# Packing the modulation rows of two to four chunks into one PSUM bank, with changed orders at block 1's passes and spare transposes ahead of block 2

## The chip, the core and the metric

The kernel runs on one core of one Trainium2 chip. The metric is the device time of one launch in microseconds (us). Three runs of the kernel before took 1881.89, 1884.19 and 1881.85 us, so the median is 1881.89 us.

## What is computed

Two blocks follow each other on 256 tokens of width 1024, everything in float32. Block 1 has two layers with a side input `ctx`, of 256 tokens too. Each layer first makes the modulation from the conditioning vectors (one for `x`, one for `ctx`), then a wide projection whose columns feed a retention branch, a differential attention branch and a gated MLP branch:

```python
for l in range(DEPTH):
    shift, scale, gate = split((silu_c @ w_mod[l] + b_mod[l]), 3)        # for x
    shift_c, scale_c, gate_c = split(silu_cc @ w_mod[l] + b_mod[l], 3)   # for ctx
    h  = rms_norm(x, g_pre[l]) * (1 + scale) + shift
    hc = rms_norm(ctx, g_pre[l]) * (1 + scale_c) + shift_c
    # ctx: projections hc @ w_in[l] (all columns in layer 0, four groups in layer 1),
    #      final retention states s_f, s_b = sum_j gamma^(..) k_j v_j^T per head
    # x:   projections h @ w_in[l], rotation of q and k, retention from s_f, s_b,
    #      differential attention over ctx keys and own keys, chunk MLP
    x = x + gate * rms_norm(merge(o_ret, o_mlp, o_diff) @ w_out[l], g_post[l])
```

Block 2 has two layers of three attention branches and a squared-ReLU MLP. The change touches of it only the transposes of `x` with which its first layer begins.

## The kernel before

**Products.** A float32 product is made of three products of parts (lines 1620, 1621 and 1622: high by high, high by low, low by high). Weights come in slabs of 256 rows by 512 columns through four slots. SyncE loads a slab into `raw`, ScalarE (ACT) rounds it to the high part `whi` (line 523), GpSimd (POOL) subtracts to get the low part `wlo` (line 498), and TensorE (PE) uses both. Four slabs make a chunk of 512 output columns for 256 tokens in two banks. Each engine has its own program, written out by hand, and waits on counting semaphores; the order of the instructions in each program is the order of the work.

**Passes.** Block 1 runs four passes: 0 is `ctx` of layer 0, 1 is `x` of layer 0, 2 is `ctx` of layer 1 (four column groups only), 3 is `x` of layer 1. Banks are named `A[0..3]` and `G[0..3]`. The slabs accumulate in `G`; `A` holds transposes, states and scores.

**Modulation.** `mod_slab` (PE, line 1739) multiplies one slab of `w_mod` with the silu of the conditioning vectors, stored two columns wide in blocks of 32 columns of zeros (`cond`). It gives two useful rows in each of four groups of 32 partitions of a bank. A chunk of `w_mod` takes four such slabs; there are 12 chunks. ScalarE copies the bank out (`mod_copy`, line 684), and `mod_turn` (line 1748) sums the row groups and turns them into columns: four products of two columns for each chunk. Chunks 0 to 3 run at the start, each in a bank of its own (`A[0], A[1], G[0], G[1]`) with its copy and its turn behind it; chunks 4 and 5 run beside pass 0's first two chunks of `w_in`, chunks 6 to 9 beside its next four, chunks 10 and 11 beside pass 1's third and fourth. The rows of chunks 6 to 11 wait in six buffers, and 24 products turn them at one place in pass 1.

**States.** In passes 0 and 2 VectorE (DVE) scales the values of four heads (`state_values`, line 1303), PE sums them per head (`sum_states`, line 1859) into four banks, and ScalarE copies each bank (line 784). In pass 0 the scaled values have room for two heads, so the third head waits for the first sum. PE waits for all four copies before the retention scores (line 1945).

**Decay matrices.** `decays` takes for each head two exponentials on ScalarE (lines 714 and 715) and three operations of 128x512 on VectorE (1282 to 1284). For layer 1, heads 0 and 1 are built at the end of pass 1, heads 2 and 3 at the end of pass 2 (ScalarE) and the start of pass 3 (VectorE).

**Edges between passes.** The normed tokens are transposed by `turn_tokens` (line 1686) in four quarters through `A[2]` and `A[3]`; ScalarE makes the high part (line 586) and VectorE the low part (1102 and 1105). Slab q of the next pass needs quarter q. Before pass 3, PE turns quarters 0 and 1 after the second and third slab of pass 2's last chunk, and 2 and 3 once both are split.

**Differential attention.** Around each of eight steps run three slabs of later columns (`late_slab`). When the fourth slab of a chunk is done, ScalarE copies two banks (line 559) before PE may start the next chunk there. ScalarE's exponentials (line 851) stand ahead of these.

**Start of block 2.** `turn_by_token` (line 1696) transposes each token tile of `x` as soon as `last_residual` has closed it (line 1147).

Of the kernel before, what the change touches and what calls it, by code (L numbers as in the profile page):

```python
# [27 lines left out]
P = 128  # L28
# [9 lines left out]
W = 512  # L38
# [47 lines left out]
def constants():  # L86
# [17 lines left out]
    pick = np.zeros((2, 2, 32, 2, 2), np.float32)  # L104
    for h in range(2):
        for a in range(2):
            pick[h, :, a, h, a] = 1
# [35 lines left out]
def build(nc, g, out):  # L143
# [14 lines left out]
    with ExitStack() as ctx:  # L158
# [73 lines left out]
        modkeep = sb_at("modkeep", [P, 4, MODN], F32, place["gate2_5"])  # L232
        modlast = sb("modlast", [P, 2, MODN])
        modkept = [modkeep[:, m] for m in range(4)] + [modlast[:, m] for m in range(2)]
# [10 lines left out]
        pick = cst["pick"].rearrange("p (h a) -> p h a", h=2)  # L245

        modw = sb("modw", [P, MODW, SLAB_K, CH])
        modrow = sb_at("modrow", [P, 4, MODN], F32, eb)
        moddrop = sb_at("moddrop", [P, 2, MODN], F32, place["aT"])
        cT = sb("cT", [P, KT, 2])  # L250
        cond = sb("cond", [P, KT, 32])
# [52 lines left out]
        OUT = [A[2], A[3]]  # L304
        UP = [[G[0], G[1]], [A[0], A[1]]]
# [207 lines left out]
        def _(act):  # L513
# [157 lines left out]
            act.activation(cond[:, :, 0:2], cT[:], ACT.Silu).then_inc(silu_c, 1)  # L671
# [9 lines left out]
            def mod_copy(bank, dst):  # L681

                act.wait_ge(mod_used, w(mod_used, SLOTS))
                act.activation(dst, bank[:, 0:MODN], ACT.Copy).then_inc(mod_copied, 1)
# [6 lines left out]
            for n, (is_x, l, full) in enumerate(PASSES):  # L691
                if n == 0:
                    act.wait_ge(ctx_in, w(ctx_in, 16))
                    norm(cx)
                    for c in range(4):
                        mod_copy((A[0], A[1], G[0], G[1])[c], modrow[:, c])
# [3 lines left out]
                stream_high(n, range(4) if n == 0 else (2, 3))  # L700
# [17 lines left out]
                if is_x:  # L718
                    pass_by(0)
                else:  # L720
                    evacuate(0, columns(z, RK), ACT.Copy)
                if n == 0:
                    mod_copy(A[2], moddrop[:, 0])
                    setup_rest()
# [25 lines left out]
                def beside_ctx_dv(s):  # L750
# [3 lines left out]
                    elif s < SLOTS - 1:  # L754
# [3 lines left out]
                        stream_high(3, (s - 1,))  # L758
# [12 lines left out]
                if n == 0:  # L771
                    mod_copy(A[3], moddrop[:, 1])
# [18 lines left out]
                if n == 0:  # L791
                    mod_copy(A[2], modkept[0])
# [6 lines left out]
                if n == 1:  # L799
                    mod_copy(A[0], modkept[4])  # L800
                if n == 2:
# [3 lines left out]
                    decays((2, 3), l)  # L805
# [4 lines left out]
                if n == 0:  # L810
                    mod_copy(A[3], modkept[1])
# [1452 lines left out]
```

## Time and profile before

| what | value |
|---|---|
| the profiled execution, its own time | 1882.96 us |
| its span | 1881.0 us |
| PE / weight loads | 98% / 81% of the span |
| POOL, ACT, DVE | 72%, 56%, 36% |
| share of the last chain that is PE's | 92% |
| DMA over the whole span | 174 GB/s; 354 and 307 GB/s in the first two of 40 slices |

The span is the stretch between the first and the last instruction of the profile; the execution's own time is some 2 us longer. Busy PE is not PE at its peak: the end of a matmul is modelled, and the rate is read from the distance of the starts. A product in float32 without parts (lines 1739, 1748, 1859, 1945) shows two records for each call, a transpose (1686, 1696, 1867) one.

### The profile page before, as it was taken

What the parts mean: (1) busy time and instruction counts of PE and PEld (TensorE: products, weight loads), DVE (VectorE), ACT (ScalarE), POOL (GpSimd) and SP (SyncE); (2) the same over time, 40 slices, a digit from 0 to 9 for tenths busy, and PEclk for the clock granted to TensorE, in tenths of its full rate; (3) what the DMA queues carried; (4) which work ended last, traced back from release to release, by engine and by line L of the source; (5) the groups of instructions that cost most, each with busy time, mean ns of one, the idle gap of its engine ahead of it and who ended that gap; (6) DMA issues with size and microseconds to landing.
All of it is one profiled execution on the core that took longest, in us unless ns stands there. A gap on an engine that the chain in (4) does not pass through costs nothing.

```text
span 1881.0 us, 26575 instructions
## 1 busy us (share of the span) xinstructions
PE 1841.7 (98%) x9988; PEld 1525.6 (81%) x9988; DVE 682.1 (36%) x1149; ACT 1045.0 (56%) x1551; POOL 1360.2 (72%) x573
## 2 busy tenths in 40 slices
PE   6999999999999999999999999999999999999998
PEld 3668888778788787878878887889998887789997
DVE  3432444512335755132434382321111745231112
ACT  3554675534667663455755666654445576645444
POOL 3567778856668778666877765778887965678886
PEclk8999999999999999999999999999999999999999
DMA  9875555754446556545555543456555654356553
GB/s 354 307 240 145 159 167 179 239 156 143 145 141 202 168 158 189 146 144 147 173 158 174 168 143 116 156 170 189 189 189 157 206 149 124 123 168 202 190 186 128
DMA packets 171416, 328.52 MB, mean 175 GB/s; under 512 B 10416, under 2 KB 15792, under 8 KB 171184
## 3 DMA queue, kind: packets, MB, share of 16 engines
q1 hardware_dynamic: 168272, 320.49, 54.8%
q10 hardware_dynamic: 3040, 6.58, 1.0%
q8 instruction: 74, 1.21, 0.3%
q14 instruction: 30, 0.25, 0.0%
HBM read 325.98 MB, written 1.05 MB: 174 GB/s over the span
## 4 chain that ended last, share of the span: by engine, by line
PE 92%; DVE 4%; ACT 2%; issue 1%; DMA 1%; SPq 0%; DVEq 0%; ACTq 0%
PE G L1620 22%; PE G L1622 21%; PE G L1621 21%; PE G L2200 2%; PE A L2202 2%; PE G L2202 2%; PE A L2201 2%; PE G L2201 2%; PE A L2200 2%; PE A L1620 2%; PE A L1621 2%; PE A L1622 2%; PE A L1981 1%; PE A L1739 1%; PE G L2004 1%
## 5 line engine op out<-in xcount | busy, mean ns | idle before, releaser
L498 POOL TENSOR_TENSOR wlo<-raw,whi 128x1024 fp32r<-128x1024 f32 (+1 forms) x568 | 1356.5, 2398 | 506.9 <-ACT whi L523 505.5
L523 ACT ACTIVATE whi<-raw 128x1024 fp32r<-128x1024 f32 (+1 forms) x568 | 594.1, 1048 | 623.7 <-PE G L1622 492.3
L1620 PE MATMUL G<-whi,hhi 128*128 128x512 f32 (+1 forms) x1488 | 597.0, 401 | 13.8 <-DVE hlo L1105 7.6
L1622 PE MATMUL G<-whi,hlo 128*128 128x512 f32 (+1 forms) x1488 | 577.6, 388 | 0.0
L1621 PE MATMUL G<-wlo,hhi 128*128 128x512 f32 (+1 forms) x1488 | 577.3, 388 | 0.0
L1620 PEld LDWEIGHTS G<-whi,hhi 128*128 128x128 f32 x1488 | 281.2, 189 | 86.0 <-issue 27.2
L1622 PEld LDWEIGHTS G<-whi,hlo 128*128 128x128 f32 x1488 | 281.1, 189 | 59.2
L1621 PEld LDWEIGHTS G<-wlo,hhi 128*128 128x128 f32 x1488 | 281.8, 189 | 50.8
L1620 PE MATMUL G<-whi,osplit 128*128 128x512 f32 x240 | 94.2, 393 | 0.0
L1621 PE MATMUL G<-wlo,osplit 128*128 128x512 f32 x240 | 93.5, 389 | 0.0
L1622 PE MATMUL G<-whi,osplit 128*128 128x512 f32 x240 | 93.4, 389 | 0.0
L1406 DVE TENSOR_REDUCE nmx<-A 128x1 f32<-128x512 f32 (+1 forms) x48 | 26.7, 597 | 135.6 <-PE A L1981 135.6
L2200 PE MATMUL G<-hhi,whi 128*128 128x256 f32 x256 | 72.5, 283 | 2.6 <-DVE hlo L1108 2.6
L2202 PE MATMUL A<-hhi,wlo 128*128 128x256 f32 x256 | 72.4, 283 | 0.0
L2201 PE MATMUL A<-hlo,whi 128*128 128x256 f32 x256 | 72.4, 283 | 0.0
L2202 PE MATMUL G<-hhi,wlo 128*128 128x256 f32 x256 | 72.4, 283 | 0.0
L2201 PE MATMUL G<-hlo,whi 128*128 128x256 f32 x256 | 72.4, 283 | 0.0
L2200 PE MATMUL A<-hhi,whi 128*128 128x256 f32 x256 | 72.4, 283 | 0.0
L559 ACT ACTIVATE z<-G 128x512 f32<-128x512 f32 x66 | 38.8, 598 | 27.1 <-PE G L1622 27.1
L1620 PEld LDWEIGHTS G<-whi,osplit 128*128 128x128 f32 x240 | 45.1, 188 | 9.5 <-issue 0.3
L1622 PEld LDWEIGHTS G<-whi,osplit 128*128 128x128 f32 x240 | 45.1, 188 | 9.5
L1621 PEld LDWEIGHTS G<-wlo,osplit 128*128 128x128 f32 x240 | 45.1, 188 | 9.0
(400 smaller groups left out, 2547.4 us busy)
## 6 DMA issues: line engine op xcount, KB each, us to landing
raw<-in_w_in SPq DMA_DIRECT2D x324, 512.0 KB, 3.7
raw<-in_w_up SPq DMA_DIRECT2D x64, 512.0 KB, 3.7
raw<-in_w_down SPq DMA_DIRECT2D x64, 512.0 KB, 3.6
raw<-in_w_out SPq DMA_DIRECT2D x40, 512.0 KB, 3.6
raw<-in_w_branch_out SPq DMA_DIRECT2D x36, 512.0 KB, 3.9
modw<-in_w_mod SPq DMA_DIRECT2D x32, 512.0 KB, 5.1
raw<-in_w_branch SPq DMA_DIRECT2D x24, 512.0 KB, 3.5
modz<-in_w_mod SPq DMA_DIRECT2D x16, 512.0 KB, 9.7
```

The source lines that it names most:

```text
L498: pool.tensor_tensor(wlo[:, s, :, 0:n], raw[:, s, :, 0:n], whi[:, s, :, 0:n].bitcast(F32), ALU.subtract)\
L523: act.activation(whi[:, slot, :, 0:n], raw[:, slot, :, 0:n], ACT.Copy).then_inc(hi_ready, 1)
L559: act.activation(dst[c][t], banks[t][:], func, scale=1.0 if scale is None else scale[t])\
L1406: ins = dve.reduce_max(nmx[:, i % 2, b:b + 1], A[2 * (i % 2) + b][:, 0:nk], AX.X, negate=True)
L1620: pe.matmul(bank, hi, whi[:, slot, kk, 0:n], start=first, stop=False)
L1621: pe.matmul(bank, hi, wlo[:, slot, kk, 0:n], start=False, stop=False)
L1622: return pe.matmul(bank, lo, whi[:, slot, kk, 0:n], start=False, stop=last)
L1739: ins = pe.matmul(bank[at:at + 32, 0:MODN], cond[:, q * SLAB_K + kk], ring[:, i % size, kk, h * MODN:(h + 1) * MODN], start=q == 0, stop=q ...
L1981: ins = pe.matmul(bank[:, c * S:(c + 1) * S], dqT[half_p, h, t * P:(t + 1) * P], kT[half_p, h], start=True, stop=True)
L2200: pe.matmul(part, high, hhi[:, k], start=k == 0 and f % 2 == 0, stop=False, skip_group_check=True)
L2201: pe.matmul(part, high, hlo[:, k], start=False, stop=False, skip_group_check=True)
L2202: ins = pe.matmul(part, low, hhi[:, k], start=False, stop=last, skip_group_check=True)
```

## The change

Chunks of `w_mod` that are copied together accumulate in one bank: chunks 0 to 3 in `G[0]`, 4 and 5 in `A[2]`, 6 and 7 in `A[3]`, 8 and 9 in `A[2]`, 10 and 11 in `A[0]`. The c-th chunk of a group reads `cond` two columns further left for each c, so its two rows land at rows 2c and 2c+1 of each group of 32, and adds to the bank. One copy and two products serve a group, each of 16 columns for four chunks and 8 for two. That makes 10 products instead of 48, and 5 copies instead of 12.

The orders that change: states go two heads to a bank, with two copies of 128x512 for four of 128x256, and the scaled values have room for four heads; PE waits for these copies one step later in pass 0. Heads 0 and 1 of layer 1's decay are finished by VectorE in pass 2 and at the start of pass 3, heads 2 and 3 after the first and third rotation of pass 3; ScalarE makes the exponentials of 2 and 3 after pass 3's first chunk. The transposes before pass 3 come one slab earlier and three quarters of them lie inside pass 2. ScalarE closes a chunk ahead of its exponentials where the chunk's last slab comes first in a step. And the first layer of block 2 gets 20 and 10 spare transposes, whose output nothing reads.

```diff
-            pick[h, :, a, h, a] = 1
+            for c in range(4):
+                pick[h, :, 2 * c + a, c, h, a] = 1
...
-                    for c in range(4):
-                        mod_copy((A[0], A[1], G[0], G[1])[c], modrow[:, c])
+                    mod_copy(G[0], modrow, 4)
...
-                stream_high(n, range(4) if n == 0 else (2, 3))
+                stream_high(n, (range(4), (2, 3), (2, 3), (3,))[n])
...
                 if is_x:
                     pass_by(0)
+                    if n == 3:
+                        decays((2, 3), l)
...
-                        stream_high(3, (s - 1,))
+                    stream_high(3, (s,)) if s < SLOTS - 1 else None
...
-                    for h in range(H1):
+                    for b, bank in enumerate(STATE_BANKS[n]):
                         act.wait_ge(state_sum, w(state_sum))
-                        act.activation(state[:, h].rearrange("p d n -> p (d n)"), A[h % 4][:, 0:2 * DK1], ACT.Copy,
+                        act.activation(state[:, 2 * b:2 * b + 2].rearrange("p h d n -> p (h d n)"), bank[:], ACT.Copy,
...
                 if n == 2:
                     act.wait_ge(x_updated, w(x_updated))
                     norm(x)
                     copy_states()
-                    decays((2, 3), l)
...
+                    closes = i < m and late % SLOTS == SLOTS - 1
+                    if closes:
+                        late_slab(late, late_dst, G[2:4])
+                        late += 1
                     if i < m:
                         act.wait_ge(diff_max, w(diff_max))
...
-                        for _ in range(2):
+                        for _ in range(1 if closes else 2):
...
-                stream_low(n, range(4) if n == 0 else (2, 3))
+                stream_low(n, (range(4), (2, 3), (2, 3), (3,))[n])
...
                 if n == 3:
-                    decays((2, 3), l)
+                    decays((1,), l)
...
-                        if h >= 2 and full:
-                            dve.wait_ge(state_sum, w(state_sum))
...
                 if n == 2:
                     residual(x)
+                    decays((0,), l)
                     dve.wait_ge(evacuated, w(evacuated, 4 * TT))
                     state_values()
                     norm(x)
-                    stream_low(3, (0, 1))
+                    dve.wait_ge(state_sum, w(state_sum, 2))
+                    stream_low(3, (0, 1, 2))
...
+                        if n == 3 and c in (0, 2):
+                            decays((2 + c // 2,), l)
...
                 if n == 1:
                     dve.wait_ge(tables_in, w(tables_in, 16 * N_TABLE[1]))
-                    decays((0, 1), 1)
...
-            def turn_by_token(src, banks):
+            def turn_by_token(src, banks, spare=(0, 0)):
...
+                    for n in range(spare[t]):
+                        k = n % KT
+                        pe.transpose(G[2 * t][:, n % 4 * P:(n % 4 + 1) * P], src[:, 0, k * P:(k + 1) * P], ident)
...
-                        ins = pe.matmul(bank[at:at + 32, 0:MODN], cond[:, q * SLAB_K + kk],
-                                        ring[:, i % size, kk, h * MODN:(h + 1) * MODN], start=q == 0,
-                                        stop=q == SLOTS - 1, skip_group_check=True)
+                        ins = pe.matmul(bank[at:at + 32, 0:MODN], cond[:, 8 + 32 * (q * SLAB_K + kk) - 2 * c:][:, 0:32],
+                                        ring[:, i % size, kk, h * MODN:(h + 1) * MODN], start=q == 0 and c == 0,
+                                        stop=q == SLOTS - 1 and c == last, skip_group_check=True)
...
-                for b in range(CH // P):
-                    h, j = divmod(b, 2)
-                    ins = pe.matmul(bank[:, at + 2 * b:at + 2 * b + 2], src[:, j * P:(j + 1) * P], pick[:, h],
-                                    start=True, stop=True)
+                turned_rows = bank[:, at:at + 8 * chunks].rearrange("p (c j a) -> p j c a", j=2, a=2)
+                for j in range(2):
+                    ins = pe.matmul(turned_rows[:, j], src[:, j * P:(j + 1) * P], pick[:, 0:2 * chunks], start=True, stop=True)
...
+                else:
+                    pe.wait_ge(h_split, w(h_split))
+                    turn_tokens(normed, HB_EDGE, (3,))
...
                         if s == 0:
-                            pe.wait_ge(state_copied, w(state_copied, H1))
                             turn_ws()
+                            pe.wait_ge(norm_ready, w(norm_ready, TT))
+                            pe.wait_ge(state_copied, w(state_copied))
...
-                            turn_tokens(normed, HB_EDGE, (s - 1,))
+                            if s == 2:
+                                pe.wait_ge(h_split, w(h_split))
+                        if s < SLOTS - 1:
+                            turn_tokens(normed, HB_EDGE, (s,))
...
-                                for b in range(6):
-                                    mod_turn(A[2], 8 * b, modkept[b], b == 5)
+                                for b in range(3):
+                                    mod_turn(A[2], 16 * b, modkept[b], last=b == 2)
...
                 if n == 0:
                     sum_states()
-                    pe.wait_ge(state_copied, w(state_copied, H1))
 
                 for i in range(H1 + 1):
+                    if n == 0 and i == 1:
+                        pe.wait_ge(state_copied, w(state_copied, 2))
+                        pe.wait_ge(mod_copied, w(mod_copied))
...
-                turn_by_token(x, HB_DOWN if l else HB_OUT)
+                if l == 0:
+                    turn_by_token(x, HB_OUT, (20, 10))
+                else:
+                    turn_by_token(x, HB_DOWN)
```

## Rows read from the trace of the kernel before

**Rows 1.** The page, its part 1: busy time, share of the span, instructions.

```profile
PE 1841.7 (98%) x9988; PEld 1525.6 (81%) x9988; DVE 682.1 (36%) x1149; ACT 1045.0 (56%) x1551; POOL 1360.2 (72%) x573
```

**Rows 2.** The waits of PE, whole span: total us, times, longest us.

```profile
PE G L1620 <- DVE hlo L1105: 7.6, 3, 5.6
...
PE G L1620 <- ACT z L559: 2.0, 4, 0.5
PE A L1686 <- DVE hlo L1105: 1.7, 1, 1.7
PE G L1620 <- DVE z L1340: 1.4, 1, 1.4
```

**Rows 3.** Windows: length, busy by engine, granted PE clock, DMA share, GB/s.

```profile
396.00:408.00 12.00, 12.00 (x69) 10.73 (x68) 0.62 (x4) 1.95 (x3) 2.81 (x2) 0.72 0.31 90
...
980.00:995.00 15.00, 11.25 (x46) 8.92 (x45) 7.61 (x16) 10.95 (x24) 9.36 (x4) 0.78 0.31 81
```

**Rows 4.** Timeline, pass 1's turns: start, us, engine, line, operation.

```profile
396.38 3.63 PE L1748 MATMUL A<-const,modkeep 128*128 128x2 f32 x32
...
402.09 0.77 PE L1620 MATMUL G<-whi,hhi 128*128 128x512 f32 x1
...
408.04 0.49 PE L1620 MATMUL G<-whi,hhi 128*128 128x512 f32 x1
...
411.26 0.48 PE L1620 MATMUL G<-whi,hhi 128*128 128x512 f32 x1
```

**Rows 5.** Timeline, pass 0's turns of chunks 4 and 5.

```profile
68.38 1.97 PE L1748 MATMUL A<-const,moddrop 128*128 128x2 f32 x16
...
68.87 0.38 ACT L684 ACTIVATE moddrop<-A 128x256 f32<-128x256 f32 x1
...
70.21 0.49 PE L1620 MATMUL G<-whi,hhi 128*128 128x512 f32 x1
```

**Rows 6.** Timelines of DVE and PE, pass 0's states and first scores.

```profile
113.91 3.80 DVE L1303 TENSOR_SCALAR e<-z,reachv 128x128 f32<-128x128 f32 x8 [9.88 <-ACT z L538]
...
129.06 0.64 PE L1739 MATMUL A<-modw,cond 128*32 128x256 f32 x8
...
131.03 1.99 PE L1859 MATMUL A<-e,z 128*128 128x256 f32 x8 [1.34 <-ACT modkeep L684]
...
136.32 1.13 PE L1945 MATMUL A<-tT 128*128 128x256 f32 x4 [0.47 <-ACT state L784]
...
137.10 0.58 PE L1620 MATMUL G<-whi,hhi 128*128 128x512 f32 x1
```

**Rows 7.** Timelines of DVE, PE and ACT around pass 2.

```profile
637.62 2.89 DVE L1283 TENSOR_TENSOR e<-e,dist 128x512 f32<-128x512 f32 x1
...
681.68 1.42 DVE L1086 TENSOR_SCALAR normed<-x,rstd 128x1024 f32<-128x1024 f32 x2
...
683.28 0.60 PE L1844 MATMUL A<-const,wsin 128*128 128x128 f32 x4
...
682.50 1.28 ACT L714 ACT_TABLE_LOAD   x1
...
686.26 1.04 ACT L523 ACTIVATE whi<-raw 128x1024 fp32r<-128x1024 f32 x1
```

**Rows 8.** Timeline of PE at the start of block 2.

```profile
983.36 1.04 PE L1696 MATMUL A<-const,x 128*128 128x128 f32 x8
...
986.75 1.09 PE L1696 MATMUL A<-const,x 128*128 128x128 f32 x8 [2.35 <-DVE x L1147]
...
989.25 0.77 PE L1620 MATMUL G<-whi,hhi 128*128 128x512 f32 x1 [1.41 <-DVE hlo L1108]
...
994.93 0.48 PE L1621 MATMUL G<-wlo,hhi 128*128 128x512 f32 x1
```

**Rows 9.** Timeline of PE at the start: two runs of eight transposes.

```profile
24.52 1.66 PE L1686 MATMUL A<-const,normed 128*128 128x128 f32 x8
...
26.02 1.04 PE L1686 MATMUL G<-const,normed 128*128 128x128 f32 x8
```

More of the change, by code:

```diff
@@ L231, in build @@
         gate2_5 = sb("gate2_5", [P, TT, CH])
-        modkeep = sb_at("modkeep", [P, 4, MODN], F32, place["gate2_5"])
-        modlast = sb("modlast", [P, 2, MODN])
-        modkept = [modkeep[:, m] for m in range(4)] + [modlast[:, m] for m in range(2)]
+        modkept = [sb_at(f"modkept{m}", [P, MODN], F32, place["gate2_5"] + m * MODN * 4) for m in range(3)]
         modT = sb("modT", [P, 2, KT, 2])
@@ L304, in build @@
         OUT = [A[2], A[3]]
+        STATE_BANKS = {0: [A[3], A[1]], 2: [A[2], A[3]]}
         UP = [[G[0], G[1]], [A[0], A[1]]]
@@ L679, in tables, with mod_copy @@
                 act.dma_start(wsins[l][:], g["mlp_w_s"][l].rearrange("a i j -> i a j")).then_inc(tables_in, 16)
-            def mod_copy(bank, dst):
-                act.wait_ge(mod_used, w(mod_used, SLOTS))
-                act.activation(dst, bank[:, 0:MODN], ACT.Copy).then_inc(mod_copied, 1)
+            def mod_copy(bank, dst, chunks=2):
+                act.wait_ge(mod_used, w(mod_used, chunks * SLOTS))
+                act.activation(dst[:], bank[:, 0:MODN], ACT.Copy).then_inc(mod_copied, 1)
             def setup_rest():
@@ L1306, in state_values @@
                         ins.then_inc(state_v, 1)
-                    dve.wait_ge(state_sum, w(state_sum, 2 if full else H1))
                 if n == 2:
                     residual(x)
+                    decays((0,), l)
                     dve.wait_ge(evacuated, w(evacuated, 4 * TT))
@@ L1732, in mod_slab @@
                 mods["n"] += 1
+                c = i // SLOTS
+                c, last = (c, 3) if c < 4 else (c % 2, 1)
                 ring, full, size = (modz, modz_full, MODZ) if i < 4 * SLOTS else (modw, modw_full, MODW)
@@ L1848, in _ @@
                     turn_ws()
-                    for c in range(2):
-                        pe.wait_ge(mod_copied, w(mod_copied))
-                        mod_turn(A[1], 8 * c, moddrop[:, c], c == 1)
+                    pe.wait_ge(mod_copied, w(mod_copied))
+                    mod_turn(A[1], 0, moddrop)
                 def sum_states():
@@ L1856, in sum_states @@
                         for t in range(TT):
-                            values = e[:, h % 2, t, 0:2 * DK1] if full else z[:, h // 2, (RQ, DQ)[h % 2]:(RQ, DQ)[h % 2] + W].rearrange(
+                            values = e[:, h % 2, t, h // 2 * 2 * DK1:(h // 2 + 1) * 2 * DK1] if full else z[:, h // 2, (RQ, DQ)[h % 2]:(RQ, DQ)[h % 2] + W].rearrange(
                                 "p (t n) -> p t n", t=TT)[:, t]
-                            ins = pe.matmul(A[h][:, 0:2 * DK1], z[:, t, RK + h * DK1:RK + (h + 1) * DK1],
-                                            values, start=t == 0, stop=t == TT - 1)
-                        ins.then_inc(state_sum, 1)
+                            ins = pe.matmul(STATE_BANKS[n][h // 2][:, h % 2 * 2 * DK1:(h % 2 + 1) * 2 * DK1],
+                                            z[:, t, RK + h * DK1:RK + (h + 1) * DK1], values, start=t == 0, stop=t == TT - 1)
+                        if h % 2 == 1:
+                            ins.then_inc(state_sum, 1)
                 def turn_group(bank, blocks):
```

58 lines of the change are left out of this document (24 added, 34 removed).

## The prediction, made before the changed kernel was run

> **What bounds the kernel now.** I read the page's busy times first [rows 1]. PE is busy 98% of the span, POOL 72%, ACT 56%. So each microsecond of PE work that goes, and each wait of PE that goes, comes off the end, as long as its suppliers keep pace; work moved on the other engines is free while PE does not wait for it. The waits of PE come second [rows 2]. After the start, where 5.6 of the 7.6 us on the low part `hlo` (line 1105) lie, the largest are few and all near the change: 2.0 us for `hlo` at the start of pass 2, 1.7 at the start of pass 3, 1.4 for the first rotation of pass 3, 2.0 for four bank copies in the attention. Third come the windows with their granted clock [rows 3]. It is 0.72 over 396 to 408 us and 0.78 over 980 to 995, so in both PE ran for a part at 1.2 GHz and for the rest at 2.4. Last I read the timelines of these places for what PE did just before [rows 4 to 9].
>
> **Part 1, pass 1's turns.** 24 products, 48 records, run from 396.38 to 402.09: 5.71 us, 0.119 each [rows 4]. Of these 12 records stay. A record of 8 moving columns instead of 2 is not in the trace. Its price lies between 0.119 us and the 0.2 us of a state product with 256 columns (eight records in 1.99 us, of which about 0.4 is the end of the last) [rows 6]; so 1.4 to 2.4 us. I take 1.4, since 8 is nearest to 2. Gain 4.3 us. Behind the turns the clock has fallen: the slab and four transposes from 402.09 to 408.04 take 5.95 us, the next slab with its transposes 3.22 (408.04 to 411.26) [rows 4]. That is 2.7 us more. Does it go? In pass 0, 16 such records took 1.97 us and the slab behind them starts with a record of 0.49 us, the length of the one at 408.04 at full clock [rows 4, 5]. So 1.97 us of narrow products did not lower the clock there, and 1.4 should not. Gain 7.0 us together.
>
> **Part 2, pass 0's turns.** Here 16 records become 4, but PE cannot take all of it. The single copy now waits for the second chunk, and that copy ran from 68.87 to 69.25 [rows 5]. With 4 records at 0.12 behind it the next slab starts at 69.8 instead of 70.21 [rows 5]. Gain 0.4 us.
>
> **Part 3, the start.** Three of the four turns there lie between slabs of `w_mod`, which arrive by DMA, and the last turn goes from 8 records to 4 (0.5 us by the price above). But `hhi` on ACT and `hlo` on DVE stand behind it together with the first weight slabs, whose transfers have not changed. I set 0, with bounds of 1.0 us worse (the first slab later because fewer products leave PE at the low clock longer) and 1.5 better (the last turn's 0.5 us and its successors in step).
>
> **Part 4, pass 0's states and scores.** Now the last modulation slab starts at 129.06, the copy holds PE 1.34 us, states of two heads run, a wait for the third head's values, two more heads, 0.47 us for the state copy, scores at 136.32 and the slab at 137.10 [rows 6]. After: nothing of this is waited for. The values of all heads are early: eight scalings took 3.80 us from 113.91 [rows 6], so sixteen end near 122, and nothing before 129 wants them. The copies are asked for one step later, behind two slabs. So PE goes from 129.7 (129.06 + 0.64) through 16 state records at 0.2 (3.2 us) and the scores (137.10 - 136.32 = 0.8) to the slab at 133.7. Gain 3.4 us.
>
> **Part 5, edges of passes 2 and 3.** The decay work of heads 0 and 1 stood on DVE ahead of pass 2's low parts. One of its six operations took 2.89 us at 637.62, while POOL ran [rows 7]; without them the 2.0 us wait [rows 2] has no cause. Head 0's three operations now come after `residual`; at 2.89 each they take up to 8.7 us, and the values they delay are needed only when the second chunk is done. Before pass 3 the quarters are turned one slab earlier, and the 1.7 us wait [rows 2] goes, since its quarter has then a whole slab of time. DVE's two decays before the first rotation become one, 8.7 us less at that price, so the 1.4 us wait [rows 2] goes. Gain 2.0 + 1.7 + 1.4 = 5.1 us. What is added: PE waits in pass 2 for the normed tokens after the first slab and the turn of `w_s`. Those are ready at 683.10 (681.68 + 1.42), and PE is there at about 683.6, after the turn that starts at 683.28 [rows 7]. It costs nothing with 0.5 us of margin; queued behind it are all later slabs. ACT gets a table load and four exponentials in pass 3, in front of its next slab: they took 3.8 us in pass 2 (682.50 to 686.26), and PE did not wait then [rows 2, 7]. Those of head 3 wait until DVE has built head 1, 8.7 us at worst. No SyncE instruction moves; POOL's order is the same, it follows ACT.
>
> **Part 6, attention.** In passes 1 and 3 a chunk's last slab comes first in two of the eight steps: four places, the four waits of 2.0 us in all [rows 2]. ACT's copies now precede its exponentials. The exponentials come later by a slab at most, and their sum is used one step (three slabs) later. Gain 2.0 us.
>
> **Part 7, spare transposes.** The eight transposes at 983.36 are followed by 2.35 us of waiting, those at 986.75 by 1.41, and then the clock is low: from 989.25 to 994.93 run 13 records in 5.68 us [rows 8]. At full clock one is 0.228 us (3.22 less 0.48 for four transposes, over 12) [rows 4], so 13 cost 2.97; the low clock costs 2.7 us. Eight transposes take 1.04 us with the end of the last in it [rows 8], some 0.11 each. Twenty take 2.2 us and fill the first gap, ten take 1.1 and lie in the second, where their successors already have their signal. If the gaps were shorter than I read, each spare transpose would cost its 0.11 us: 0.3 us in all if the first gap is overrun. Do they hold the clock? At the start PE's clock was low at 24.52 (eight transposes in 1.66 us) and full for the eight at 26.02 (1.04 us) [rows 9]; so a run of transposes, behind narrow products, did raise it. I take the 2.7 us as gained.
>
> The Trainium skill speaks against this part: "TensorE: Matmul & The Clock Gate", Part 4 (PE-mode transpose), says that full clock does not engage for transposes, which do not count as PE activity in the same way. By that rule the sum would lose this term. The two runs at 24.52 and 26.02 speak against the rule, though slabs stood just before them.
>
> **The sum.** 7.0 + 0.4 + 0 + 3.4 + 5.1 + 2.0 + 2.7 = 20.6 us. The profiled execution took 1882.96 us for a span of 1881.0, so it would be near 1862.4. It was 1.07 us above the median of 1881.89, and the median after should be 1861.3 us, 1.1% less.
>
> **The rivals.** *The spare transposes do not hold the clock.* For it: they are half as dense in columns as a slab, and eight plus eight of them did not hold it [rows 8]. Against it: the gaps were open then, and rows 9. Everything else holds: 1861.3 + 2.7 + up to 0.3, or 1864.2.
>
> *New waits take the place of the old ones in block 1's last passes.* The 0.5 us margin on the normed tokens is thin, and ACT's moved exponentials stand before slabs while DVE's operations run at 2.89 instead of 0.7 us when POOL is busy [rows 7]. The 5.1 us of part 5 come back, and 1 us of part 4: 1867.4.
>
> *The start turns well or the clock falls at other places.* The three runs before lie 2.3 us apart, which is about one such stretch of low clock. At best 1857 with 1.5 us at the start and one low stretch less.
>
> *The change does not do what it says:* the waits are put down to the wrong releaser, and behind each stands another (a slab's low part from POOL). Then only the products' own 4.7 us of parts 1 and 2 go, less new waits of 2: about 1879.
>
> *Slower.* ACT's program stops in pass 3 ahead of its slab until DVE has built head 1, and all four heads' decays come onto the path that way or behind the rotations: 12 operations at 2.89, 35 us, less some 3 us of slab in store (the 3.8 us that did no harm in pass 2). 1861.3 + 32 = 1893. It decides only where these waits exceed 20.6 us; up to the slack nothing is seen. Against it: DVE idles between the rotations, since each waits for a chunk of four slabs.
>
> **How the numbers follow.** Forecast with all parts 0.52; spare transposes without effect 0.24; new waits 0.13; a better start 0.05; not what it says 0.04; slower 0.02. Only the last lies above 1881.89, and 0.2% of it, 3.8 us, is about what a measurement of this kernel can tell from no change; 1879 lies within. So faster 0.94, same 0.04, slower 0.02. The forecast's own range is 1858.5 to 1863.5 (bounds of part 3, 1.0 us for wider products, one clock stretch). With the second and third case the range is 1857 to 1868.
>
> **What would show it.** Line 1748 has 20 records instead of 96, and in pass 1 the next slab starts with a record near 0.49 us, not 0.77. Pass 0's first late slab starts 4 us after its last modulation slab, not 8. PE waits on lines 1686, 1620 (`hlo` near 650, `z` of line 1340) and 1859 are gone, and none over 0.5 us comes at the move of `norm_ready`. After the spare transposes the first slab of block 2 starts with a record near 0.5 us, not 0.77. The prediction is wrong if POOL or a transfer stands behind PE at one of these places, if the clock falls elsewhere, or if the start grows longer.

## The result and the profile after

The changed kernel takes 1865.82 us (median of four runs, 1864.62 to 1865.95), the kernel before on the same chip 1881.87 us. The ratio is 0.991, with a 95% interval of 0.990 to 0.992: 16.05 us less. The forecast was 1861.3, so 4.5 us of the expected gain are missing. The profiled execution took 1864.62 us for a span of 1862.7, against 1882.96 and 1881.0. The measured time lies above the range of 1858.5 to 1863.5 that the forecast gave for itself, and within the range of 1857 to 1868 that takes in two of its rivals. By the spans the gain is 18.3 us; the profiled execution before lay 1.1 us above its median, that after 1.2 us below. The accounts below are made in the spans. The lines have moved: the slab products are now lines 1619 to 1621, `mod_slab` 1743, `mod_turn` 1752, `sum_states` 1860, `turn_tokens` 1685, `turn_by_token` 1695 and its spare transposes 1700, `hlo` 1103 and 1106, `state_values` 1299.

The waits of PE over the whole span (total us, times, longest us), to be read beside [rows 2]:

```profile
PE G L1619 <- DVE hlo L1103: 6.1, 1, 6.1
PE A L1860 <- DVE z L1299: 3.9, 1, 3.9
...
PE G L1619 <- DVE hlo L1106: 1.7, 2, 1.3
```

The four waits for bank copies, the quarter's wait before pass 3, the rotation's wait and the 2.0 us for `hlo` at the start of pass 2 are gone. One wait of 3.9 us is new: the state sums of pass 2 wait for the scaled values. Here are the places of the change in the timeline of PE (start, us, engine, line, operation, what it waited for), to be read beside [rows 4, 5, 6, 8]:

```profile
68.48 0.61 PE L1752 MATMUL A<-const,moddrop 128*128 128x8 f32 x4 [0.75 <-ACT moddrop L684]
68.95 0.49 PE L1619 MATMUL G<-whi,hhi 128*128 128x512 f32 x1
...
127.80 0.64 PE L1743 MATMUL A<-modw,cond 128*32 128x256 f32 x8
128.37 3.72 PE L1860 MATMUL A<-e,z 128*128 128x256 f32 x16
131.93 1.03 PE L1951 MATMUL A<-tT 128*128 128x256 f32 x4
132.60 0.58 PE L1619 MATMUL G<-whi,hhi 128*128 128x512 f32 x1
...
391.91 1.40 PE L1752 MATMUL A<-const,modkept 128*128 128x8 f32 x12
393.17 0.48 PE L1619 MATMUL G<-whi,hhi 128*128 128x512 f32 x1
...
396.36 0.48 PE L1619 MATMUL G<-whi,hhi 128*128 128x512 f32 x1
...
661.23 1.02 PE L1860 MATMUL A<-z 128*128 128x256 f32 x4
666.18 4.26 PE L1860 MATMUL A<-z 128*128 128x256 f32 x12 [3.93 <-DVE z L1299]
670.10 0.58 PE L1619 MATMUL G<-whi,hctx 128*128 128x512 f32 x1
...
684.25 0.48 PE L1619 MATMUL G<-whi,hhi 128*128 128x512 f32 x1
...
968.73 2.35 PE L1700 MATMUL G<-const,x 128*128 128x128 f32 x20
...
972.17 1.25 PE L1700 MATMUL G<-const,x 128*128 128x128 f32 x10
973.74 0.47 PE L1619 MATMUL G<-whi,hhi 128*128 128x512 f32 x1 [0.32 <-DVE hlo L1106]
```

Where the time went is read by the start of the same PE instruction in both traces, and the lead grown between two of them:

| from one place to the next | before | after | lead grows by | forecast |
|---|---|---|---|---|
| first slab of pass 0 | 37.16 | 37.16 | 0 | 0 |
| its last modulation slab beside `w_in` chunk 1 | 67.32 | 66.51 | 0.81 | 0 |
| slab behind pass 0's turns | 70.21 | 68.95 | 0.45 | 0.4 |
| first late slab of pass 0, behind the states | 137.10 | 132.60 | 3.24 | 3.4 |
| slab behind pass 1's turns | 402.09 | 393.17 | 4.42 | 4.3 |
| next slab (the low clock) | 408.04 | 396.36 | 2.76 | 2.7 |
| states of pass 2 (attention copies, `hlo`) | 677.09 | 661.23 | 4.18 | 1.0 + 2.0 |
| slab behind these states | 680.36 | 670.10 | **-5.60** | 0 |
| second slab of pass 3 (the quarter) | 696.45 | 684.25 | 1.94 | 1.7 |
| slab behind the first rotation | 744.92 | 730.98 | 1.74 | 1.4 |
| first slab of block 2 (attention copies) | 989.25 | 973.74 | 1.57 | 1.0 |
| to the end (the low clock) | 1881.0 | 1862.7 | 2.8 | 2.7 |

Eleven rows lie at the forecast, within 0.2 us below it, or above it, and one gives 5.6 us back, at a place where the sum had put nothing. Its window (length, busy us of PE, PEld, DVE, ACT and POOL with their counts, granted clock, DMA share, GB/s) shows that PE was at the low clock for part of it:

```profile
661.23:670.10 8.87, 4.94 (x18) 3.79 (x16) 7.96 (x15) 4.62 (x8) 4.62 (x2) 0.81 0.69 207
```

### The profile page after: what moved, and what is told of

It is laid out like the page before. It is cut to its first block, busy times and chain, and to the rows that moved or that the text cites. A ratio compares the mean times of both kernels' runs of the same rounds, so it can differ in the third digit from the quotient of the medians.

```text
span 1862.7 us, 26472 instructions
## 1 busy us (share of the span) xinstructions
PE 1829.0 (98%) x9942; PEld 1515.8 (81%) x9942; DVE 692.3 (37%) x1149; ACT 1042.5 (56%) x1540; POOL 1360.2 (73%) x573
## 3 DMA queue, kind: packets, MB, share of 16 engines
HBM read 325.98 MB, written 1.05 MB: 176 GB/s over the span
## 4 chain that ended last, share of the span: by engine, by line
PE 94%; DVE 2%; DMA 1%; ACT 1%; issue 1%; SPq 0%; DVEq 0%; ACTq 0%
PE G L1619 23%; PE G L1621 22%; PE G L1620 22%; PE G L2209 2%; PE A L2211 2%; PE A L2210 2%; PE G L2211 2%; PE G L2210 2%; PE A L2209 2%; PE A L1619 2%; PE A L1620 2%; PE A L1621 2%; PE A L1987 1%; PE G L2010 1%; PE A L1743 1%; PE A L1673 1%
```

## The experiments

Each kernel is the changed one with one edit, if nothing else is said. The kernel before was timed on the same chip beside each group: 1882.18 us beside e1 to e4, 1881.96 beside e5 to e8 and 1882.08 beside e9 to e11.

### Why pass 2 gave 5.6 us back

DVE's timeline in pass 2, changed kernel. The three operations of head 0's decay stand at 639.66 to 647; then come the scalings:

```profile
644.31 2.77 DVE L1282 TENSOR_TENSOR decay<-e 128x512 f32<-128x512 f32 x1
651.18 16.52 DVE L1299 TENSOR_SCALAR z<-z,reachv 128x128 f32<-128x128 f32 x16 [4.10 <-ACT z L538]
```

And POOL's, which runs without a gap from 636.13 to 665.85:

```profile
636.13 29.72 POOL L498 TENSOR_TENSOR wlo<-raw,whi 128x1024 fp32r<-128x1024 f32 x12 [4.20 <-ACT whi L523]
```

In the kernel before, the same sixteen scalings started at 667.04 and took 11.93 us. How many of them are done in a stretch is read from the windows of that line alone (length, DVE busy and count, clock, DMA share, GB/s). A window counts every operation that touches it, so one that crosses an edge is counted on both sides:

```profile
651.18:653.50 2.32, 2.32 (x2) 1.00 0.78 224
653.50:656.00 2.50, 2.50 (x2) 1.00 0.73 224
...
663.20:665.85 2.65, 2.65 (x2) 0.96 0.84 242
665.85:667.70 1.85, 1.84 (x10) 0.50 0.73 214
```

The seven windows from 651.18 to 667.70 (the three not shown count two each) count 22 operations, and each of their six inner edges is crossed by one. So seven of the sixteen scalings start while POOL runs, one for each of its operations, and the other nine follow in 1.85 us once POOL has stopped. The timeline from 651.75 shows two of the slow ones:

```profile
651.70 4.81 DVE L1299 TENSOR_SCALAR z<-z,reachv 128x128 f32<-128x128 f32 x2
```

The kernel before had a gap of POOL from 667.23 to 668.03. Five scalings start in the 1.03 us up to its end. In the 7.35 us of three POOL operations behind it four start, three of which take 2.4 to 2.5 us each; the fifth that this window counts crosses its edge:

```profile
667.00:668.03 1.03, 0.99 (x5) 1.00 0.70 265
668.03:675.38 7.35, 7.35 (x5) 1.00 0.63 177
```

*Theory:* beside POOL each of DVE's short operations lasts as long as the POOL operation next to it, and POOL ran dry less, because PE no longer stood still for 2.0 us at the pass's start. *Rival:* head 0's decay, moved ahead of the scalings, simply delays them.

**Head 0's decay behind the norm** (e3_decay0_later).

```diff
                     residual(x)
-                    decays((0,), l)
                     dve.wait_ge(evacuated, w(evacuated, 4 * TT))
                     state_values()
                     norm(x)
+                    decays((0,), l)
```

> Head 0's three decay operations on VectorE move from ahead of pass 2's 16 value scalings to behind the norm of x. Two causes are told apart for the new wait of 3.9 us of the state products for the scalings (16.5 us where they took 11.9 before). Theory A (POOL runs without a gap because PE's wait at the start of pass 2 is gone, and each pair of scalings waits for a 2.4 us subtraction): the wait stays at 3 to 4 us, span 1862 to 1863. Theory B (the decay operations ahead slow POOL and push its work into the scalings): scalings near 12 us, the wait gone, span near 1857.5.

Measured: 1863.08 us (1862.85 to 1864.17), 2.7 less than the changed kernel. The scalings still took 15.63 us from 652.09, beside eleven POOL operations in a row (26.14 us from 637.03), one gap of POOL of 0.79 us (663.17 to 663.95), in which four scalings start, and one more operation. PE's waits were 2.7 us in two:

```profile
663.40 1.96 PE L1860 MATMUL A<-z 128*128 128x256 f32 x8 [1.10 <-DVE z L1299]
666.99 1.99 PE L1860 MATMUL A<-z 128*128 128x256 f32 x8 [1.62 <-DVE z L1299]
```

So the moved decay explains a part of the loss, the smaller one of the waits (3.9 to 2.7). The rest stays with the decay out of the way. That the clock no longer fell beside the shorter waits (16 records in 3.95 us of work, against 4.26 us for the last 12) makes up the other part of the gain.

**Four scalings in place of sixteen** (e4_four_scalings). The same values, in four operations of 128x512 with a broadcast factor:

```diff
+                    if not full:
+                        dst4 = z[:, :, RQ:RQ + 4 * W].rearrange("p a (b c n) -> p a b c n", b=2, n=DK1)
+                        for t in range(TT):
+                            for d in range(2):
+                                ins = dve.tensor_tensor(dst4[:, :, :, 2 * t + d], ..., ALU.mult)
+                        ins.then_inc(state_v, H1)
+                        return
```

> Pass 2's 16 scalings of 128x128 become four tensor_tensor operations of 128x512 with a broadcast factor. Theory A (what costs is that every second operation waits for a subtraction of POOL): four operations take at most 4 x 2.9 = 11.6 us, more likely 6 to 9, ready before PE asks 10 us after the copy; the 3.9 us wait and the slow state products behind it go, 5.6 us in all, span near 1857.1. Rival (something else stands ahead of the state products, x_updated or the transfers): the wait stays, span near 1862.7.

Measured: 1860.86 us (1860.21 to 1861.27), 5.0 less than the changed kernel. DVE and PE:

```profile
651.87 9.47 DVE L1298 TENSOR_TENSOR z<-z,reachv 128x512 f32<-128x512 f32 x4 [4.11 <-ACT z L538]
```

```profile
661.92 3.61 PE L1871 MATMUL A<-z 128*128 128x256 f32 x16
665.18 0.58 PE L1630 MATMUL G<-whi,hctx 128*128 128x512 f32 x1
...
669.51 0.66 PE L1696 MATMUL A<-const,normed 128*128 128x128 f32 x4 [0.81 <-DVE normed L1084]
```

The first took 1.05 us and the other three 2.9 each, one to a POOL operation, with the decay still ahead of them. A short scaling beside POOL had taken 2.4. So it is the number of operations that cost, much more than their columns. The wait is gone, and what was next late is the thing the prediction had given 0.5 us of margin: the normed tokens, by 0.8 us. The span of 1858.8 us is 1.7 above the 1857.1 expected: 1.0 at the normed tokens, and 0.7 at the start, where the clock rose later than in the changed kernel's profile.

**The decays back at the end of pass 1** (e5_decays_back). This puts the 2.0 us wait back:

```diff
-                if n == 3:
-                    decays((1,), l)
...
                     residual(x)
-                    decays((0,), l)
...
                     dve.wait_ge(tables_in, w(tables_in, 16 * N_TABLE[1]))
+                    decays((0, 1), 1)
```

> VectorE builds the decays of heads 0 and 1 at the end of pass 1 again, as in the kernel before; nothing of them is left in pass 2 or at the start of pass 3. All else is the changed kernel's. Theory A (GpSimd without gaps): the wait of 2.0 us for hlo at the start of pass 2 comes back and lets GpSimd run dry once per slab, so its subtractions there stand in groups with gaps between; the 16 scalings take some 12 us instead of 16.5, TensorE doesn't wait 3.9 us for them, and the state records don't run at the low clock. That is 5.6 us gained for 2.0 lost: about 1862.3, although a wait was put back. Theory B (only the three decay operations ahead of the scalings matter): without them 2.7 us are gained, as when they stood behind the scalings (1863.1), and the returned wait costs 2.0: about 1865, with scalings still near 15.6 us and a wait for them of 1 to 2.7 us. If the scalings' length has nothing to do with either, the time is 1867.8.

Measured: 1861.98 us (1861.39 to 1862.54), 3.8 *less* than the changed kernel, with a wait more in it; theory A had 1862.3. PE, then POOL, then DVE:

```profile
636.06 0.47 PE L1617 MATMUL G<-whi,hhi 128*128 128x512 f32 x1 [1.77 <-DVE hlo L1103]
...
663.92 3.61 PE L1858 MATMUL A<-z 128*128 128x256 f32 x16
```

```profile
643.98 7.35 POOL L498 TENSOR_TENSOR wlo<-raw,whi 128x1024 fp32r<-128x1024 f32 x3 [0.17 <-ACT whi L523]
651.65 2.40 POOL L498 TENSOR_TENSOR wlo<-raw,whi 128x1024 fp32r<-128x1024 f32 x1 [0.33 <-ACT whi L523]
654.86 7.35 POOL L498 TENSOR_TENSOR wlo<-raw,whi 128x1024 fp32r<-128x1024 f32 x3 [0.81 <-ACT whi L523]
```

```profile
653.87 11.92 DVE L1297 TENSOR_SCALAR z<-z,reachv 128x128 f32<-128x128 f32 x16 [9.07 <-ACT z L538]
```

POOL's gaps are back, the scalings take 11.92 us as before the change, and the state sums run in 3.61 us with no wait. There are five between 636.21 and 665.74, three of them in the lines above, and they sum to 2.45 us, near the 2.0 us that PE now waits. In the head-0 experiment the decay was out of the way too, but POOL had one gap of 0.79 us up to its last operation beside the scalings, and they took 15.63. The pair says that about 3.7 us of the scalings' length hang on POOL's gaps. That PE's wait makes these gaps is argued from their sum and not shown by itself: the edit brings the wait back by putting the decays at the end of pass 1, and no run has the wait alone. The Trainium skill has a rule that bears on this: "SBUF — State Buffer", section "Who interferes with whom", says that DVE and GpSimd share one pair of ports, and that a DVE instruction in a 2-port mode, which `tensor_scalar` can enter, contends for it with GpSimd: whichever issues first holds the pair for its whole instruction while the other blocks. The trace agrees: each of the seven slow scalings ends 0.08 or 0.09 us after a POOL operation does.

**Both cures of pass 2 together** (e6_four_and_later): the edits of the first two experiments.

> Both edits that helped pass 2 at once: four scalings of 128x512 for sixteen short ones, and head 0's decay behind the norm instead of ahead of the scalings. With the four scalings alone PE still waits 0.8 us for the normed tokens (one operation of 3.0 us beside GpSimd). Theory A: the scalings were no longer waited for, so only that 0.8 us is left to gain, if the norm comes earlier by the decay's three operations (7.5 us): 1860.0. Theory B (each operation ahead of PE's supply counts): also 1860. If the decay operations behind the norm delay the low part that pass 3's first slab needs, a wait for hlo of up to 1 us comes and the time is 1861 to 1862.

Measured: 1859.62 us (1859.33 to 1860.46), where 1860.0 was expected, a ratio of 0.988 (0.987 to 0.990) to the kernel before and 6.2 us below the changed kernel. It is the fastest version. Of PE's waits at this place 0.5 us on the scaled values is left, none on the normed tokens:

```profile
PE A L1871 <- DVE z L1298: 0.5, 1, 0.5
```

### Narrow products and the clock

**The turns of pass 1 twice and four times** (e7_turns_x2, e8_turns_x4). The same six products are repeated, with the same outcome:

```diff
-                                for b in range(3):
-                                    mod_turn(A[2], 16 * b, modkept[b], last=b == 2)
+                                for b in range(3 * 4):
+                                    mod_turn(A[2], 16 * (b % 3), modkept[b % 3], last=b == 3 * 4 - 1)
```

> The six products (12 records) that turn the rows in pass 1 are run twice, with the same result: 24 records of 8 columns. If narrow records lower the clock only after a long run of them (the kernel before: 48 records over 5.7 us did, 16 over 2.0 us in pass 0 did not), 24 over some 2.6 us are between: a first record of the slab behind near 0.49 us means no fall, and the sum is only 1.3 us over the changed kernel; 0.77 means a fall, and 4 us over it. I expect no fall, at 0.11 us for each record.

> The six products are run four times: 48 records, as many as before the change but 8 columns wide and not 2. If the count of narrow records sets both costs (prediction, part 1), they take 5.2 to 5.7 us, the slab behind starts with a record of 0.77 us and takes some 2.7 us longer: 4.2 + 2.7 = 6.9 us over the changed kernel, 1872.7. If the wider records hold the clock, only 4.2 us: 1870.0.

Measured: twice 1868.07 us in its one run, four times 1872.67 us (1872.44 to 1873.12), 6.85 over the changed kernel where 6.9 was expected. PE at twice, then at four times:

```profile
392.52 2.74 PE L1752 MATMUL A<-const,modkept 128*128 128x8 f32 x24
395.12 0.48 PE L1619 MATMUL G<-whi,hhi 128*128 128x512 f32 x1
```

```profile
391.83 6.70 PE L1752 MATMUL A<-const,modkept 128*128 128x8 f32 x48
398.39 0.77 PE L1619 MATMUL G<-whi,hhi 128*128 128x512 f32 x1
```

The price is that of the record, not of its columns: 24 took 2.60 us from their start to the slab's, 0.108 each. Those of two columns had 0.119 each [rows 4], but that figure has the fall of the clock in it: record by record, both widths start 0.111 us apart before the fall and 0.213 us apart behind it. Behind 24 the slab starts at full clock (0.48), behind 48 at the low one (0.77). The 48 took 6.56 us and not 5.2, because the clock fell while they ran: the window from 396 to 400 shows 0.50, that from 393 to 396 still 0.95. So both halves of part 1 hang on the number of records, and 48 narrow records in a row lower the clock though PE is never idle, at 8 columns as at 2. The single run of twice lies 2.25 us above the changed kernel's median, not 1.3, and its span 3.4 us above the changed kernel's: 0.6 us stood there before the turns began (392.52 against 391.91), 1.3 came at the turns, and some 1.4 behind pass 2's wait, where the clock stayed low for 6.8 us and not 3.4.

### The spare transposes

**Without them** (e1_no_spare) **and with narrow products in their place** (e2_narrow_spare). The second fills the same time with products of two columns, whose output nothing reads:

```diff
-                    turn_by_token(x, HB_OUT, (20, 10))
+                    turn_by_token(x, HB_OUT, (10, 5))
...
-                        pe.transpose(G[2 * t][:, n % 4 * P:(n % 4 + 1) * P], src[:, 0, k * P:(k + 1) * P], ident)
+                        pe.matmul(G[2 * t][:, 2 * n:2 * n + 2], src[:, 0, k * P:(k + 1) * P], cst['pick'][:, 0:2], start=True, stop=True)
```

> The changed kernel without the 30 spare transposes. Theory (transposes hold the clock): the first 13 or so products of block 2 run at 0.43 us instead of 0.23, and the span is 2.7 us longer than the 1862.7 of the changed kernel, near 1865.4; nothing else moves. Rival (transposes do not count as activity, and the clock stayed up in the changed kernel by chance): no low stretch behind the gap, span within 0.5 us of 1862.7.

> The 20 and 10 spare transposes are replaced by 10 and 5 products of two columns (20 and 10 records of about 0.12 us, so PE's queue is filled for the same time). Theory (what holds the clock is columns through the array): the clock falls as without spares, span near 1865.4 with 13 records of 0.43 us behind it. Rival (any issued work in the gap holds it, weight loads too): span near 1862.7.

Measured: 1868.68 us (1867.18 to 1869.62) without them, 2.9 over the changed kernel; 1867.46 (1867.01 to 1867.53) with the narrow ones, 1.6 over it by the medians and 2.6 by the spans (1865.3). Followed at the same PE instruction, the place itself costs 2.9 us without the spares (974.12 to 981.62, where the changed kernel goes from 973.74 to 978.36) and 2.8 us with the narrow products. The span without them is 5.0 us longer, though, and not 2.7: near 1002 PE waits 1.1 us for POOL's low part, a wait that neither the kernel before nor the changed one has and that the expectation had not put in. What brings it was not tried. PE with the narrow ones, and then the window without any and the same window of the changed kernel:

```profile
968.60 2.29 PE L1700 MATMUL G<-const,x 128*128 128x2 f32 x20
...
972.03 1.48 PE L1700 MATMUL G<-const,x 128*128 128x2 f32 x10
973.60 0.77 PE L1619 MATMUL G<-whi,hhi 128*128 128x512 f32 x1
```

```profile
974.00:980.00 6.00, 5.88 (x14) 4.66 (x15) 2.49 (x7) 4.00 (x10) 0.86 (x1) 0.50 0.33 96
```

```profile
974.00:980.00 6.00, 6.00 (x28) 4.94 (x28) 2.11 (x6) 4.52 (x10) 1.97 (x2) 1.00 0.27 80
```

Narrow products that keep PE as busy as the transposes do not hold the clock; the transposes, of 128 columns, do. The rival of the prediction that took the side of the Trainium skill ("TensorE: Matmul & The Clock Gate", Part 4) is thereby refuted for this place.

What is shown is that transposes hold a clock that is up. That they raise one that is low is not shown. At the start of the changed kernel the two runs that the prediction took from [rows 9] as evidence stood wholly at the low clock, 0.213 us from one transpose to the next, and the clock rose only behind them, at 27.36 (in e3, with the same start, it rose within the second run):

```profile
23.65 1.97 PE L1685 MATMUL A<-const,normed 128*128 128x128 f32 x8
25.41 1.91 PE L1685 MATMUL G<-const,normed 128*128 128x128 f32 x8
```

**The spare transposes alone, in the kernel before** (e9_before_spare).

> The kernel before, with nothing changed but the 20 and 10 spare transposes at the start of block 2. If transposes hold the clock by themselves there (theory A, from the run with the narrow products in their place), the first slab starts with a record near 0.5 us at 989.2 and the slabs up to 995 run at full clock: 2.7 us gained, 1879.2. If the gain in the changed kernel came from its other edits (theory B), or by the Trainium skill's rule that transposes do not count as activity: no change, 1881.9, or up to 0.3 us slower.

Measured: 1879.48 us (1879.19 to 1882.03) against 1882.08, a ratio of 0.9989 (0.998 to 0.9998), 2.6 us. The clock in the window of [rows 3] is 1.00 where it was 0.78, and the first slab of block 2 starts with a record of 0.47 us:

```profile
988.21 0.47 PE L1620 MATMUL G<-whi,hhi 128*128 128x512 f32 x1 [0.31 <-DVE hlo L1108]
```

So the gain is theirs and needs nothing of the rest of the change.

### The two orders that went as forecast

**State copies waited for at once in pass 0** (e10_states_wait).

```diff
                     sum_states()
+                    pe.wait_ge(mod_copied, w(mod_copied))
+                    pe.wait_ge(state_copied, w(state_copied, 2))
...
-                    if n == 0 and i == 1:
-                        pe.wait_ge(state_copied, w(state_copied, 2))
-                        pe.wait_ge(mod_copied, w(mod_copied))
```

> The changed kernel, but in pass 0 PE waits for both state copies and for the rows' copy straight behind the states, as before the change, and not one step later. The second copy ran from 132.13 to 132.73 while the scores began at 131.93: the scores come 0.8 us later (part 4: the moved wait is worth 0.8 of its 3.4 us, the other 2.6 come from the merged values, banks and copies), 1866.6. If the moved wait carried the whole of part 4, it is 3.3 us, 1869.1; if the order doesn't matter, 1865.8.

Measured: 1866.69 us (1866.50 to 1867.58), 0.9 over the changed kernel. PE at the scores, and at pass 2's states:

```profile
132.73 1.10 PE L1950 MATMUL A<-tT 128*128 128x256 f32 x4 [0.78 <-ACT state L784]
...
667.01 5.49 PE L1860 MATMUL A<-z 128*128 128x256 f32 x12 [3.89 <-DVE z L1299]
```

The moved wait is worth 0.8 of part 4's 3.2 us; the merged chunks, values and banks have the rest by difference, and were not tried one by one. Its span is 2.0 us longer, not 0.9. The second line shows where the other part lies: the same wait of 3.9 us as in the changed kernel, but the twelve records behind it took 5.49 us and not 4.26, because the clock stayed low for 6.8 us and not 3.4.

**ScalarE's exponentials ahead of the closing slab again** (e11_no_close).

```diff
-                    closes = i < m and late % SLOTS == SLOTS - 1
+                    closes = False
```

> The changed kernel with ScalarE's exponentials ahead of the chunk's last slab again in all attention steps. The four waits of 0.4 to 0.5 us on the copies of a closed chunk come back: 2.0 us in four (part 6), 1867.8. If the copies were late for another reason, or the slack of the exponentials had been spent elsewhere, less than 1 us and under 1866.8.

Measured: 1867.87 us (1867.47 to 1870.35), 2.05 over the changed kernel; the four waits are back. Its span is 3.2 us longer; followed at the same PE instruction, the four places cost 0.67, 0.76, 0.76 and 0.76 us, where the list says 0.5 each.

```profile
PE G L1619 <- ACT z L559: 2.0, 4, 0.5
```

## Why the prediction was right, and where not

Every product and every wait that the prediction named went, and the clock rose where it was to. The number did not come by that working alone: at one place 5.6 us were given back, and waits that were worth more than forecast made up for 2.3 us of it. Without these 2.3 the time would have been near 1868, at the edge of the wide range. The forecast's own range was also narrower than the bounds it was said to be made of: 1.0 us each for part 3 and the wider products and one clock stretch of 2.3 would have reached 1865.6.

**Part 1** held in both terms. The record of 8 columns costs 0.108 us, the lower end of the bounds was the right one, and the low clock went with the count of records. **Part 2** gave 0.45 for 0.4, **part 4** 3.24 for 3.4, of which the moved wait is 0.8. Its sign, the first late slab 4 us after the last modulation slab, was too small against its own sum of 4.6; it came 4.8 us after (127.80 to 132.60).

**Part 3** was 0 up to the first slab, within its bounds. The rows' columns were ready early, and DVE's low part began at 35.13 and not at 36.32, but it took 1.89 us and not 0.69, because it now lay beside a POOL operation that ran until 36.46 (36.40 before). The 0.81 us behind it come from the clock, which rose earlier: the windows from 41 to 42 us (before, then after) show 0.50 and 0.99. This was luck of one execution: e3, e4 and e7 have the changed kernel's start, and in their traces the clock stays low until 42.2 to 43.0 us and PE is 0.6 to 0.9 us later at this place.

```profile
41.00:42.00 1.00, 1.00 (x4) 0.71 (x3) 1.00 (x2) 0.00 (x0) 1.00 (x2) 0.50 0.98 403
```

```profile
41.00:42.00 1.00, 1.00 (x8) 0.55 (x11) 0.96 (x3) 0.02 (x1) 1.00 (x1) 0.99 0.95 373
```

**Part 5** has the step that failed: "the values they delay are needed only when the second chunk is done". The deadline was right, and the margin was not worked out: the sixteen scalings of pass 2 have no price in the prediction. They had 11.93 us in the kernel before and no wait of PE behind them [rows 2], but the last ended at 678.98, when PE's sums had already run since 677.09, so there was little to spare. And this length was that of a DVE beside a POOL with gaps. With PE's 2.0 us wait away the gaps were gone, the same sixteen took 16.5 us, PE waited 3.9 us, and its clock fell behind that: 5.6 us given back. A wait that is removed also feeds the engines behind it, and here one of them blocks the supplier of the next stage. "New waits" was a rival at 1867.4, the nearest to what came. It had DVE's slow operations beside POOL, but named the normed tokens and ACT's exponentials as the places, not the scalings, and not that POOL would lose its gaps. The margin on the normed tokens held in the changed kernel only because PE came late; once the scalings were mended it was missed by 0.8 us.

**The waits that went** were worth more than their listed length. The wait for `hlo` is 2.03 us in two in the list; with the decays back, PE went from the slab at 628.59 (628.49 in the changed kernel) to the states at 663.92 and not 661.23, 2.6 us more. The other waits show the same in the table of leads: attention 1.57 for 1.0, rotation 1.74 for 1.4, quarter 1.94 for 1.7. That is 0.2 to 0.35 us for each wait. The list counts idle time from the end of the last record, which lasts 0.39 us while the next could start 0.23 after it; so 0.16 of each stall is shown as work, and the first record behind it takes 0.30 us to the next start and not 0.23 (636.06 to 636.36 with the decays back). Together parts 5 and 6 gave 9.4 us for the 7.1 forecast.

**Part 7** held: followed at the same PE instruction, the place is worth 2.9 us without the spares, 2.8 with narrow products in their stead and 2.8 with the spares alone in the kernel before. By the medians the three are 2.9, 1.6 and 2.6. Of its grounds, that from [rows 9] did not repeat.

The sum in the spans: 20.6 forecast, plus 0.8 at the start, plus 2.3 for waits longer than listed, less 5.6, makes 18.1; measured are 18.3. The remaining 2.3 us to the 16.05 of the medians are the difference between single executions, which lie up to 2.3 us apart in the kernel before. The traces show two places that can make it: the low clock at the start ends before 41.6 us or after 42.1 us (0.6 to 0.9 us), and behind pass 2's wait it lasts 3.4 or 6.8 us (1.2 to 1.5 us). The profiled execution of the changed kernel has the short one at both places. Of the six other traces that have pass 2's wait of 3.9 us, e7, e8 and e10 have the long one behind it, so the loss there is not always 5.6 us. What sets them was not tried.

## What to carry to other kernels

Before you take a wait of PE away, list what ran on the other engines during it, and how much each had to spare. Where DVE and POOL work side by side, DVE's length in the profile belongs to POOL's present rhythm, and it has to be priced again with POOL running without a gap. Many short DVE operations there cost by their number: four of 128x512 in 9.5 us did the work of sixteen of 128x128 in 16.5. Where PE must stand for a few us at full clock (here 2.35 and 1.41), transposes nobody reads kept it, and narrow products didn't.

## What the runs showed of the hardware

- Narrow products alone lower TensorE's clock without any idle time: 48 records of 8 columns fell to the low clock while running (6.56 us, window clock 0.50 at the end), 24 did not (2.60 us, one run). Records of 2 and of 8 columns cost the same, 0.111 us at full clock and 0.213 at the low one. Products of two columns in place of the spare transposes left the next slab at 0.77 us for its first record.
- Spare transposes of 128 columns did hold it (granted clock 1.00 for 0.50 over 974 to 980), in two kernels. Sixteen at the low clock ran 3.6 us at the start of the changed kernel (23.65 to 27.25) without raising it before their end.
- Beside fp32 subtractions of 128x1024 on POOL (2.4 us each), DVE finished one scaling for each of them, of 128x128 (2.4 us) as of 128x512 (2.9, POOL's then 2.8); nine of the short ones took 1.85 us once POOL was idle.
- A stall of PE cost 0.2 to 0.35 us more than the profile's idle time (0.76 for 0.5, 2.6 for 2.03 in two).
